# Narrow matmuls paired across parts of the array, and weight low parts subtracted in four pieces

## What is computed

```python
h = RMSNorm(x); P = h @ W_in
y_A = HGRN2(P_A); y_B = DSA(P_B); y_C = RWKV7(P_C); y_D = FoX(P_D)
m = sum_n sigmoid(P_gate_n) * (y_n @ W_branch_n)
x = x + RMSNorm(m @ W_out)
x = x + RMSNorm(relu(RMSNorm(x) @ W_up)**2 @ W_down)
```

## Time and profile before

| what | value |
|---|---|
| median of 3 runs | 2381.36 us (2374.36 to 2382.37) |
| the profiled execution, its own time | 2384.08 us |
| its span in the trace | 2382.3 us |
| PE busy | 2224.7 us, 93% of the span |
| DVE, ACT, POOL busy | 42%, 32%, 35% |
| mean granted TensorE clock | 0.954 of full speed |

### The profile page before, as it was taken

One profiled execution on the slowest core, in us unless ns is written; L12 is line 12 of the kernel. 1 busy time (PEld: TensorE's weight loads), 2 busy tenths in 40 slices (PEclk: granted clock), 3 DMA queues, 4 the chain that ended last, 5 costly groups with the idle time before them and its releaser, 6 DMA issues.

```text
span 2382.3 us, 30841 instructions
## 1 busy us (share of the span) xinstructions
PE 2224.7 (93%) x10760; PEld 1708.4 (72%) x10760; DVE 1002.9 (42%) x1690; ACT 770.3 (32%) x1178; POOL 824.3 (35%) x379
## 2 busy tenths in 40 slices
PE   7999998899999899999989898979999998999996
PEld 5875755788667688888768657657877676888884
DVE  5525757432323243134275359383222333332243
ACT  5332334212433432222362333341224325222224
POOL 3212322311325544446523214131113265444463
PEclk9899999899899899999989899988999999999998
DMA  4111211000112222322212112110002122222222
GB/s 153 63 61 46 80 45 45 27 28 28 53 45 80 71 89 97 97 97 97 90 51 80 54 45 89 36 45 27 28 28 68 38 82 71 98 97 97 97 97 97
DMA packets 50348, 161.69 MB, mean 68 GB/s; under 512 B 5280, under 2 KB 13600, under 8 KB 49952
## 3 DMA queue, kind: packets, MB, share of 16 engines
q1 hardware_dynamic: 49056, 157.05, 20.2%
q10 hardware_dynamic: 1152, 2.86, 0.4%
HBM read 157.79 MB, written 2.10 MB: 67 GB/s over the span
## 4 chain that ended last, share of the span: by engine, by line
PE 62%; issue 18%; DVE 11%; POOL 7%; ACT 2%; DVEq 0%; POOLq 0%; DMA 0%; ACTq 0%; SPq 0%
PE bank L546 15%; PE bank L547 13%; PE bank L548 13%; POOL w_lo L1378 5%; DVE slab L1646 2%; PE bank L652 2%; PE bank L638 2%; PE bank L863 2%; PE bank L851 2%; PE bank L859 2%; PE bank L767 2%; DVE col L1640 2%; PE bank L700 1%; POOL w_lo L1351 1%; PE bank L666 1%
## 5 line engine op out<-in xcount | busy, mean ns | idle before, releaser
L1351 POOL TENSOR_TENSOR w_lo<-w_raw,w_hi 128x1024 fp32r<-128x1024 f32 x156 | 384.8, 2468 | 1123.2 <-ACT w_hi L1001 1122.4
L546 PE MATMUL bank<-hn_hi,w_hi 128*128 128x512 f32 x1312 | 564.5, 430 | 47.6 <-DVE tmp L1472 24.0
L547 PE MATMUL bank<-hn_lo,w_hi 128*128 128x512 f32 x1312 | 525.7, 401 | 0.0
L548 PE MATMUL bank<-hn_hi,w_lo 128*128 128x512 f32 x1312 | 525.1, 400 | 0.0
L1378 POOL TENSOR_TENSOR w_lo<-w_raw,w_hi 128x1024 fp32r<-128x1024 f32 x128 | 311.1, 2433 | 370.7 <-ACT w_hi L1313 370.7
L546 PEld LDWEIGHTS bank<-hn_hi,w_hi 128*128 128x128 f32 x1312 | 255.0, 194 | 159.4 <-issue 68.4
L546 PE MATMUL bank<-u_hi,w_hi 128*128 128x512 f32 x736 | 299.4, 407 | 28.1 <-POOL w_lo L1345 11.5
L548 PEld LDWEIGHTS bank<-hn_hi,w_lo 128*128 128x128 f32 x1312 | 254.5, 194 | 56.3
L547 PE MATMUL bank<-u_lo,w_hi 128*128 128x512 f32 x736 | 289.6, 394 | 0.0
L548 PE MATMUL bank<-u_hi,w_lo 128*128 128x512 f32 x736 | 289.2, 393 | 0.0
L547 PEld LDWEIGHTS bank<-hn_lo,w_hi 128*128 128x128 f32 x1312 | 256.0, 195 | 45.8 <-issue 4.4
(11 more groups left out here) (313 smaller groups left out, 3079.5 us busy)
## 6 DMA issues: line engine op xcount, KB each, us to landing
w_raw<-wrest SPq DMA_DIRECT2D x144, 512.0 KB, 3.3
w_raw<-wmerge SPq DMA_DIRECT2D x80, 512.0 KB, 3.5
w_raw<-wproj SPq DMA_DIRECT2D x64, 512.0 KB, 3.4
x<-x_in SPq DMA_DIRECT2D x4, 512.0 KB, 7.1
slab<-rope ACTq DMA_DIRECT2D x2, 1024.0 KB, 4.8
out<-x SPq DMA_DIRECT2D x4, 512.0 KB, 2.6
con<-tables SPq DMA_DIRECT2D x1, 898.0 KB, 11.2
slab<-masks SPq DMA_DIRECT2D x1, 896.0 KB, 12.9
```

The source lines that it names most:

```text
L546: mm(o_, stat[0], mov[0], start=first, stop=False)
L547: mm(o_, stat[0], mov[1], start=False, stop=False)
L548: return mm(o_, stat[1], mov[0], start=False, stop=last)
L1351: pool.tensor_tensor(wlo[:, s_, :], wraw[:, s_, :], whi[:, s_, :].bitcast(f32), SUB).then_inc(*w_split.up())
```

## The change

The order of narrow matmuls is changed so that two heads (in the index scores four) that lie in different parts of the array alternate. No matmul is added or left out.

- Attention: logits, outputs and their waits go by pairs of heads (8 pairs and no longer 16 heads); transposes stay single. DVE's and ACT's programs for it are reordered to fit. The dense steps at each place stay.
- Index scores: four heads at once into banks 4 to 7, after all four relus of the group before, then four dense steps. The wait for the copied index weights (which lie in bank 7) moves ahead of them.
- Mixer A and C: the loops in lines 688 to 735, 827 to 840, 867 to 871 and 884 to 895 are turned inside out, so that the two heads of a pair alternate at each kind of matmul.
- POOL makes each low part in four instructions of 256 columns and no longer in one of 1024; the semaphore rises after the last.

```diff
-                    def logits(i):
-                        b, h = divmod(i, H)
-                        lo = (h % 2) * HD
+                    def logits(p):
+                        b, t = divmod(p, FT)
                         n = (b + 1) * P
-                        if i >= 2:
-                            pe.wait_ge(*at_mx.at(L, base + i - 1))
+                        if p:
+                            pe.wait_ge(*at_mx.at(L, base + 2 * p))
+                        for side in range(2):
+                            lo = side * HD
+                            ins = mm(ps[4 + side][:, 0:n], q[lo:lo + HD, t, b * P:(b + 1) * P], k[lo:lo + HD, t, 0:n],
+                                     start=True, stop=last)
...
+                    def outputs(p):
+                        b, t = divmod(p, FT)
+                        pe.wait_ge(*at_pt.at(L, base + 2 * p + 2))
...
+                        for j in range(b + 1):
+                            for side in range(2):
+                                i, h = 2 * p + side, 2 * t + side
+                                ins = mm(ps[7][side * HD:(side + 1) * HD, o0:o0 + P], v[:, j, h * HD:(h + 1) * HD],
+                                         S(pt + i % 4 // 2, i % 2)[:, j * P:(j + 1) * P], start=j == 0, stop=j == b)
...
+                    for p in range(8):
+                        if p + 1 < 8:
+                            logits(p + 1)
+                        dense(("bd"[which] + "_att", 2 * p, 0))
+                        transposed(2 * p)
+                        dense(("bd"[which] + "_att", 2 * p, 1))
+                        if p:
+                            outputs(p - 1)
+                        dense(("bd"[which] + "_att", 2 * p + 1, 0))
+                        transposed(2 * p + 1)
+                        dense(("bd"[which] + "_att", 2 * p + 1, 1))
+                    outputs(7)
...
@@ mixer A, levels: banks pair and pair + 1 alternate @@
-                    for b in range(4):
-                        lo = (b % 2) * HD
+                    for pair in (0, 2):
                         if lv:
-                            pe.wait_ge(*a_sc_used.at(L, (lv - 1) * NT + b + 1))
+                            pe.wait_ge(*a_sc_used.at(L, (lv - 1) * NT + pair + 2))
                         for i in range(4):
...
+                            for b in (pair, pair + 1):
...
@@ index scores @@
+                    for t in range(2):
+                        if n_ix:
+                            pe.wait_ge(*b_relu.at(L, n_ix))
+                        for j in range(4):
+                            lo = j * IDIM
+                            mm(ps[4 + j][:, 0:(b + 1) * P], S(11)[lo:lo + IDIM, t, b * P:(b + 1) * P],
+                               S(0, 1)[lo:lo + IDIM, 0:(b + 1) * P], start=True, stop=True).then_inc(*b_ix.up())
+                        n_ix += 4
                         dense(("b_ix", n_ix - 1))
...
@@ mixer C, pairwise products: sides 0 and 1 alternate, the third group waits for two masks @@
                         if i >= 4:
-                            pe.wait_ge(*c_mu.at(L, 6 * c + i - 3))
+                            pe.wait_ge(*c_mu.at(L, 6 * c + 2))
...
@@ mixer C, right-hand side @@
+                    for t in range(FT):
+                        for side in range(2):
+                            lo = side * HD
+                            mm(ps[7 if side == 0 else 4][:, t * HD:(t + 1) * HD], AA[lo:lo + HD, t, cs], st[lo:lo + HD, t, :],
+                               start=True, stop=False)
+                        for side in range(2):
+                            h = 2 * t + side
+                            ins = mm(ps[7 if side == 0 else 4][:, t * HD:(t + 1) * HD], MTm[:, h * P:(h + 1) * P],
+                                     tm[2][:, c, h * HD:(h + 1) * HD], start=False, stop=True)
...
@@ ACT in attention @@
+                    exps(0)
+                    exps(1)
+                    for p in range(8):
+                        transposed(2 * p)
+                        if p + 1 < 8:
+                            exps(2 * p + 2)
+                            exps(2 * p + 3)
+                        if p % FT == 0 and p:
+                            attn_out(which, p // FT - 1)
+                        transposed(2 * p + 1)
...
@@ POOL, at lines 1351 and 1378 @@
-                    pool.tensor_tensor(wlo[:, s_, :], wraw[:, s_, :], whi[:, s_, :].bitcast(f32), SUB).then_inc(*w_split.up())
+                    for n in range(4):
+                        cs = slice(n * W, (n + 1) * W)
+                        ins = pool.tensor_tensor(wlo[:, s_, cs], wraw[:, s_, cs], whi[:, s_, cs].bitcast(f32), SUB)
+                    ins.then_inc(*w_split.up())
...
@@ DVE in attention @@
+                    masked(0)
+                    masked(1)
+                    for p in range(8):
+                        for i in (2 * p, 2 * p + 1):
+                            probs(i)
+                        if p + 1 < 8:
+                            masked(2 * p + 2)
+                            masked(2 * p + 3)
+                        for i in (2 * p, 2 * p + 1):
+                            gated(("bd"[which] + "_att", i, 1))
+                        if p % FT == 0 and p:
+                            out_lo(p // FT - 1)
```

More of the change, by code:

```diff
@@ L645, in outputs @@
[L645 to L661, removed]
+                        for side in range(2):
+                            lo = side * HD
+                            ins = mm(ps[4 + side][:, 0:n], q[lo:lo + HD, t, b * P:(b + 1) * P], k[lo:lo + HD, t, 0:n],
+                                     start=True, stop=last)
+                            if last:
+                                ins.then_inc(*at_lg.up())
@@ L668, in attention @@
                         ins.then_inc(*at_tr.up())
[L669 to L672, removed]
+                    def outputs(p):
+                        b, t = divmod(p, FT)
+                        pe.wait_ge(*at_pt.at(L, base + 2 * p + 2))
+                        if t == 0 and (b >= 2 or which):
+                            pe.wait_ge(*at_o.at(L, which * NT + b - 1))
+                        o0 = b % 2 * 256 + t * P
+                        for j in range(b + 1):
[3 more added lines that the diff above has]
+                                         S(pt + i % 4 // 2, i % 2)[:, j * P:(j + 1) * P], start=j == 0, stop=j == b)
+                        if t == FT - 1:
+                            ins.then_inc(*at_pv.up())
+                    logits(0)
+                    for p in range(8):
[10 more added lines that the diff above has]
+                    outputs(7)
                 enter()
@@ L1109, in transposed, with exps @@
                         take(("bd"[which] + "_att", i, 1))
-                    for i in range(16):
-                        b, h = divmod(i, H)
-                        n = (b + 1) * P
+                    def exps(i):
+                        n = (i // H + 1) * P
                         buf = S(6 + i % 4 // 2, i % 2)
@@ L1377, in lo_ahead @@
                     pool.wait_ge(*w_hi_done.at(L, q * 16 + (MLP_CHUNK0 + j + AHEAD + 1)))
-                    pool.tensor_tensor(wlo[:, s_, :], wraw[:, s_, :], whi[:, s_, :].bitcast(f32), SUB)\
-                        .then_inc(*w_split.up(times))
+                    for n in range(4):
+                        cs = slice(n * W, (n + 1) * W)
+                        ins = pool.tensor_tensor(wlo[:, s_, cs], wraw[:, s_, cs], whi[:, s_, cs].bitcast(f32), SUB)
+                    ins.then_inc(*w_split.up(times))
                 with pool.Fori(0, QUARTERS - 1) as q:
@@ L1670, in probs, with masked @@
                         ts(buf, buf, col[:, 6, i % 4:i % 4 + 1], None, MUL).then_inc(*at_p.up())
-                    for i in range(16):
+                    def masked(i):
                         b, h = divmod(i, H)
```

111 lines of the change are left out of this document (49 added, 62 removed).

## The result

| | before | changed |
|---|---|---|
| median | 2381.86 us (2374.36 to 2389.37, 4 runs) | 2224.23 us (2223.14 to 2225.13, 4 runs) |
| profiled execution: time, span | 2384.08, 2382.3 | 2224.35, 2222.5 |
| mean granted clock | 0.954 | 0.964 |
| PE waits over 0.15 us, summed over the trace, without the 11.4 us before the first matmul | 126 us | 142 us |

The ratio is 0.9343, interval 0.9321 to 0.9365: 157.6 us faster, where 132 were forecast (2250; range 2210 to 2312). The range holds it, but two of its terms were wrong: the low parts (a loss of 3 forecast, a gain of 13.7 measured) and the clock (3 forecast, 14 measured in mixer C alone). They come to some 28 us together.

The account below looks back on a forecast made before the run. PE, busy 93% of the span, was taken as the bound, with the order of narrow matmuls improvable. Savings of 10 + 11.5 + 31.8 + 58.4 + 22 = 133.7, less 3, plus 3, from 2384.1 gave 2250 us, range 2210 to 2312.

Parts of the forecast that it names:

- A, levels: Mixer A, line 700: 32 passes take 1.9 us instead of 2.53, 0.63 saved in each of 16 levels, 10 us.
- A, chunks: Mixer A's chunks: eight groups of two passes become four of four, 2.88 to 1.45 us, 11.5 us over 8 chunks.
- index scores: Index scores four heads at once: first to last relu 25.9 us, from 43.4 and 40.2; 31.8 us saved.
- attention: Four attention stages: a pair costs one head's slot; logits 5.9, outputs 5.5, switches 3.2, together 14.6 each, 58.4 us saved.
- C, outputs and state: Mixer C: right-hand side saves 0.93 us, outputs and state 1.8, per chunk; 8 x 2.73 = 22 us.
- C, pairwise products: Mixer C, line 838: shorter on PE, but DVE's masks set the solve's start, so nothing gained or lost.
- That rival (2265 to 2324): Attention and index scores: streams don't run side by side, wholly (2324) or for four quarters (about 2265 to 2290); chance 0.15.
- The Trainium skill's 3.07x for four tiles: Index scores: packing four 32-row tiles gives 3.07x, not 4x; group 1.37 us, not 1.05, 4 us more over 12 groups.
- Heads that share a bank: Rival, lines 728 and 887: row halves writing one bank take turns, costing 0.2 us a pair; 2257, chance 0.10.
- ACT and DVE hold the index scores: Rival: two buffers hold each index-score group, 5.2 us a group, 14 us less gain, 2264; chance 0.15.
- the POOL step: Low parts in four pieces: a loss of 3 us, between a loss of 10 and a gain of 10.
- The clock term: Granted clock, low after line 870's alternating groups, which halve: 3 us gain, between 15 lost and 15 gained.

Follow-up runs that it names:

- as the last edit: Changed kernel against the same kernel with low parts in one instruction again: that one measured 2237.92 us, 13.7 slower, 12.6 by the ratios.
- both kernels with the step in the gap: Changed kernel with one dense step put into PE's 1.38 us wait per mixer C chunk: 2225.35 us; the same plus MLP low parts whole: 2224.92.

## Why the prediction was right, and where it was wrong

| step | forecast | measured, and by what |
|---|---|---|
| A, levels | 10 | 8.8 (67.2 to 62.7 or 62.8 in each layer, both with pieces) |
| A, chunks | 11.5 | 11.3 |
| index scores | 31.8 | 27.6 alone, 35.2 with the pieces |
| attention | 58.4 | 54.8 |
| C, outputs and state | 22 | 22.6 at full clock |
| C, pairwise products | 0 | 0 |
| pieces | -3 | +13.7 as the last edit; +19.5 alone, but there with mixer C's clock in it |
| clock | +3 | 14 in mixer C (345.8 less 331.9); 28.5 in all by the estimate |

**The array's time was right.** The slots were added up from steps of 0.11 and a switch, and each came out within 0.1 us: 1.93 for 1.90, 1.47 for 1.45, 1.80 for 1.86, 2.37 for 2.4. A level's period fell from 8.24 to 7.60, the 0.63 foreseen; the stage gave 0.6 a layer less, since PE waits 0.3 at one level and 0.3 longer after the last, both for DVE. Attention gave 54.8 and not 58.4. By slots in the traces before and of attention alone, logits gave 5.7 in B and 6.1 in D (5.9 forecast), outputs 5.5 (5.5), and transposes and dense steps between them 2.7 to 3.2 (3.2). The rest is mainly PE's waits, 0.3 to 0.7 a stage longer, of which the prediction had counted 0.3 once.

**Streams do run side by side**, also where no row had shown it: two of 512 columns, and four quarters. That rival (2265 to 2324) falls by the slots of 1.06 and 1.07. The Trainium skill's 3.07x for four tiles (TensorE: Matmul & The Clock Gate, Part 3) would have made the latter 1.37, an estimate from it and the 1.05 of one head; it is not seen here.

**Heads that share a bank do not take turns.** Lines 744 and 914 write one bank from two halves of the rows; four passes take 0.37, as line 742's on halves of the columns do. Had they taken turns, 0.2 a pair would be missing, and neither 1.47 nor 2.37 has room for it. The restriction that the prediction cited from the Trainium skill, TensorEngine Tiling (Array Packing), does not show in the time of these two lines.

**ACT and DVE hold the index scores** only a little: a group of 512 columns is 4.61 long (206.18 to 210.79) for 4.05 forecast, 5.2 in the rival. The groups took 3.59, 4.16 and 4.61 where PE's work alone was put at 3.6, 3.8 and 4.05; what had been added for ACT and DVE was more than that, so 23.5 from first to last relu came out below 25.9.

**The step that failed is the POOL step.** The prediction saw that the two engines take turns, and that one DVE instruction waits 0.6 for a piece and not 2.1. On the POOL side its price was of the right size: with the pieces alone PE's waits for POOL grow by 10.0 us. But the places were others: the wait at 59 us, which it took for the plainest, is 4.65 for 4.49, and the one in preparation of C is 6.20 for 3.03. What it put too low is the other side. It gave back 1 to 2 us at 416.62, and PE's waits for DVE fall by 12.3 alone and by 11.8 as the last edit. Three of these places stood in the trace of before, with DVE as the releaser of PE's wait and a DVE instruction at twice its length or more beside a low part just ahead of it: line 754 (4.50), line 816 (3.05) and one level of mixer A (2.48). The fourth, behind the index scores, did not: the kernel before waits nothing there in layer 0 and 1.33 in layer 1, and the gain of the pieces appears only once the scores are grouped. And it had nothing for what followed: the clock falls behind some of these waits, so a gain in waits of 1.7 alone, or 7.8 as the last edit, came with 16.7 and 9.6 of clock by the estimate. How much of the clock's part the pieces cause is not shown, above all the 13.9 in mixer C.

**The clock term was too small.** It was right that the alternating groups go with the low clock, but 3 us had been taken for both signs, between 15 lost and 15 gained. Over the whole kernel the clock gave 28.5 by the estimate, outside these bounds. The 14 in mixer C could have been read from the trace of before: four chunks of mixer C there take 41.5, the other four 42.9 to 47.2, together 14 us more. That the index scores of layer 0 took 43.4 from first to last relu and those of layer 1 40.2 was the clock too (0.95 and 1.00 over the stretch).

The measured terms, with the pieces as the last edit, add to 152.8, for 157.6 in the medians. The 19.5 of the pieces alone can't be put in their place, though the sum would look better for it (158.6): its profiled execution has the chunks of mixer C at 331.9 us, the very number from which the 14 of the clock comes, so that gain would stand in the sum twice. Both misses have one sign, and the range held the time since it reached 40 below the forecast.

## What to carry to other kernels

Order narrow matmuls so that neighbours use different parts of the array; add up the slots of one part and a switch, and the result is good to 0.1 us. When POOL and DVE take turns, a long instruction of the one costs at every place where PE waits for the other: look for DVE instructions at more than their undisturbed length on the chain in front of each wait, and cut the long one. Compare repeated periods of one loop first, since what the clock costs stands in their differences. And before the gains of single experiments are added up, look in their traces whether two of them hold the same stretch.

## What the runs showed of the hardware that was not expected

- Passes on four 32-row quarters, 512 columns each, started 0.007 us apart, and eight of them took 1.07 us, as two did.
- Two row halves writing one bank ran side by side: four passes of 128 columns in 0.37 us.
- POOL and DVE wait for each other by whole instructions: 1.23 us of DVE became 1.75 beside 256-column pieces, and 3.38 beside 1024 columns; a piece of 0.73 became 1.70.
- The granted clock of mixer C fell to half in some chunks with alternating head-by-head groups (21 of 48 in six profiles, 0 of 8 in the profile of the pieces alone), and in none of 40 chunks with pairs. In both kernels with the step in the gap it fell in the fourth chunk of layer 1, where PE had run out of dense work, and not in the fourth chunk of layer 0, where it had too.
- A few us of waiting can cost more by the clock than by themselves: behind a wait of 4.51 the clock was at half for 3.4 us, and behind one of 2.75 it stayed full; but behind 2.74 it fell once and once not.
